# Recurrent branch: the order of TensorE's work in the state stage, around the norms and at the group starts

## The chip, the cores and the metric

The kernel runs on one core of a Trainium2 chip. The metric is the device time of one launch in microseconds (us); lower is better. The core's engines run separate instruction streams and meet at semaphores: PE is TensorE (matmuls), DVE is VectorE, ACT is ScalarE, POOL is GpSimd, SP issues most DMAs.

## The reference

Two layers of a hybrid trunk over 640 tokens (512 of a sample, 128 of a prompt), width 1024. Each layer projects its input, runs three branches (a recurrent one, gated linear attention, latent attention), merges them and projects back. The change lies in the recurrent branch, whose core is

```python
def step(s, inp):
    r_t, w_t, k_t, v_t, kk_t, a_t = inp
    sa = jnp.einsum('bhij,bhj->bhi', s, -kk_t)
    s = (s * w_t[:, :, None, :] + sa[..., None] * (kk_t * a_t)[:, :, None, :]
         + v_t[..., None] * k_t[:, :, None, :])
    return s, jnp.einsum('bhij,bhj->bhi', s, r_t)
...
o = outs[0] + outs[1]                      # two directions
mu = jnp.mean(o, -1, keepdims=True)
var = jnp.mean(jnp.square(o - mu), -1, keepdims=True)
o = (o - mu) * lax.rsqrt(var + RW_GN_EPS)
...
bonus = jnp.sum(r * k * r_k, -1, keepdims=True) * v
```

## The kernel before

The recurrence is computed in chunks of 128 tokens. A layer loops over 4 **pairs** of heads (p); each pair handles 5 **steps** (s = 0 to 3 of the sample, s = 4 the prompt), in both directions at once, in three **groups**: (0, 1), (2, 3) and (4,). Every engine's stream is written out by hand in one order; nothing is scheduled by a planner. Only PE's stream is touched by the change.

A pair goes like this on PE:

- **Opening.** `sums("kkss")` reduces the squared keys; it waits for `dve_kksq`, which DVE makes at the end of its work on the pair before. Projections of later inputs (`BESIDE[p]`, `project`, 8 weight tiles each) follow.
- **Group start.** `turns(s)` transposes B, K (result TB) and A, v (result TA) of a step; `scores(s, "Ab", B_)` and `scores(s, "Ak", K_)` make two score tiles of two PSUM banks each. DVE masks Ab twice: a small copy into XX (signal `dve_XT`, L1578) and two full copies (L1551), after which Ab's banks are free; it masks the XX parts of both steps first, then all of the first step's Ab, then the second step's Ab, then the first step's Ak. PE transposes XX back (result X, waits for `dve_XT`), and squares it (X2, X4, X8 ...), a chain that ACT and DVE empty from PSUM.
- **Solving.** V1, V2, V3, then Ya, Ye, Yb, each with an ACT or DVE copy between.
- **State stage.** For each step: TaT (a transpose), U (waits for `dve_state`, the running state), the state update S and the output O. S and O are sums over several matmuls; `open_outputs(s)` issues their first terms ahead, at a place where PE would wait. After the O of step 0 and of step 2, `turns` of the next group's first step is issued.
- **Closing.** `bonus`, `omean` and `ovar` are three norm sums, `ovar` waits for `dve_osq`, the squares that DVE makes from `omean`. Then comes the next pair's first projection, then the next `kkss`. After `ovar` ACT takes a logarithm and an exponential, and DVE five products and then the next pair's scaled keys and their square (`dve_kksq`).

`beat(r)` (r = 0 to 11) issues pieces of other projections in the prompt's group.

PSUM has 8 banks. `ticket` hands them out in a ring, in program order; banks of open sums are held and passed over. The matmul that takes a bank waits until the engine that reads the bank's last content is done with it. PE runs in order, so whatever is behind such a matmul waits as well. An order of matmuls is thus also an assignment of banks.

Of the kernel before, what the change touches and what calls it, by code (L numbers as in the profile page):

```python
# [30 lines left out]
P = 128  # L31
# [149 lines left out]
def build(nc, a, seen):  # L181
# [4 lines left out]
    with ctx:  # L186
# [311 lines left out]
        def _(pe):  # L498
# [103 lines left out]
            for l in range(DEPTH):  # L602
# [8 lines left out]
                pe.wait_ge(act_tanh.sem, act_tanh[l])  # L611
                for p in range(PAIRS):

                    project(l, BESIDE[p][0])
# [11 lines left out]
                    for steps in GROUPS:  # L626
# [78 lines left out]
                        def open_outputs(s):  # L705

                            TA, TB = B(s, "TA", 2), B(s, "TB")
                            got(s, ("TB", "act"))
                            opened["S", s] = ticket(pe, ("S", l, p, s), 1, "dve") if s != 3 else None
                            for d in range(2) if s != 3 else ():  # L710
                                mm(psum[:, opened["S", s] + P * d:opened["S", s] + P * d + P], TB[:, 2 * d + 1, :],
                                   TA[:, d, :], d == 0, False)
# [5 lines left out]
                            book["held"] |= {opened[k, s] // 512 for k in "SO" if opened[k, s] is not None}  # L718
# [23 lines left out]
                        for s in steps:  # L742
                            if s in (0, 1, 3):
                                turns(s)
                        for s in steps:
                            scores(s, "Ab", B_)
                        scores(steps[0], "Ak", K_)
                        beat(0)
                        for s in steps:
# [7 lines left out]
                            last.then_inc(filled.sem, filled.mark(("X", l, p, s)))  # L757
                        for s in steps:
# [55 lines left out]
                        open_outputs(steps[0])  # L814
# [5 lines left out]
                        for s in steps:  # L820
                            got(s, ("Ya", "act"), ("Ya", "dve"))
                            halves64(s, "Ye", "dve", 0, carried)
                        beat(10)
                        for s in steps:
                            got(s, ("Ye", "dve"))
                            halves64(s, "Yb", "act dve", 1, solved)
                        for s in steps:
# [8 lines left out]
                        for s in steps:  # L836
                            K, TA, TB = B(s, "K"), B(s, "TA", 2), B(s, "TB")
                            U = K[:, 2:4, :] if s != 4 else B(s, "J")[:, 2:4, :]
                            if s != 4:
# [9 lines left out]
                                if s + 1 in steps:  # L849
                                    open_outputs(s + 1)  # L850
                                got(s, ("U", "dve"))
                            at, s_at = opened["O", s], opened["S", s]
# [1185 lines left out]
```

## Time and profile before

| | us |
|---|---|
| median of 3 runs | 2876.14 (2874.84 to 2878.2) |
| the profiled execution: its time | 2874.18 |
| its span | 2872.4 |
| PE busy in the span | 2693.6 (94%) |
| DVE busy, ACT busy | 1180.9 (41%), 854.2 (30%) |
| recurrent branch, layer 0 | about 142 to 775 of the span |
| recurrent branch, layer 1 | about 1573 to 2138 of the span |

Where PE is idle inside its span, the profile names the engine whose signal ended the idle time. "Granted clock" is the share of 2.4 GHz that TensorE got; 0.50 is its lower level, 1.2 GHz.

### The profile page before, as it was taken

Reading aid. Unit: us, or ns where it says so; the run is one execution under the profiler, and the core shown is the slowest. Engines: PE = TensorE matmul, PEld = TensorE weight load, DVE = VectorE, ACT = ScalarE, POOL = GpSimd, SP = SyncE. Lnnn points to the kernel's source line nnn. Section 1 sums busy time; section 2 is a strip of 40 time slices with the busy share of each in tenths; the row PEclk is TensorE's granted clock in tenths of the full one; section 3 lists DMA queues with packets and bytes.
Section 4 is the critical chain, followed back from the end, with each engine's and each line's share of the span. In section 5 each row is a group of like instructions: output and inputs, shape, how many; then the busy total and the mean of one; then the engine's idle time right before and its main releaser. Section 6 shows DMA issues by size and latency. Waiting matters only on the chain.

```text
span 2872.4 us, 49516 instructions
## 1 busy us (share of the span) xinstructions
PE 2693.6 (94%) x21716; PEld 1726.2 (60%) x21716; DVE 1180.9 (41%) x2329; ACT 854.2 (30%) x1366; POOL 33.8 (1%) x62
## 2 busy tenths in 40 slices
PE   8999999999988999999999999999998899999997
PEld 2585756657555665555555858585755556555554
DVE  1452626454275454211134545454547644421112
ACT  1332314242244444200013232323324444420000
POOL 0000000000000000000000000000000000000000
PEclk9999999999999999999999999999999999999998
DMA  8101011020200100222231010101010010012221
GB/s 324 52 10 68 24 40 52 15 77 2 76 23 23 35 16 23 89 72 67 84 99 59 2 40 9 39 10 32 17 32 23 23 35 15 23 54 67 73 76 62
DMA packets 35844, 140.79 MB, mean 49 GB/s; under 512 B 4592, under 2 KB 4624, under 8 KB 35120
## 3 DMA queue, kind: packets, MB, share of 16 engines
q1 hardware_dynamic: 31968, 116.74, 12.6%
q0 software_dynamic: 3664, 20.88, 2.1%
q8 instruction: 175, 2.87, 0.4%
q14 instruction: 37, 0.30, 0.0%
HBM read 130.62 MB, written 6.98 MB: 48 GB/s over the span
## 4 chain that ended last, share of the span: by engine, by line
PE 82%; DVE 9%; ACT 6%; issue 2%; DMA 1%; POOL 0%; ACTq 0%; DVEq 0%; SPq 0%; POOLq 0%
PE psum L500 79%; PE psum L503 2%; DVE tmp L1401 1%; DVE tmp L1404 1%; DVE m_nm L1876 1%; DVE tmp L1412 1%; ACT tmp L1373 1%; DVE tmp L1578 1%; DVE acts L1401 1%; DVE tmp L1551 1%; ACT tmp L1126 1%; DVE acts L1404 1%; DMA ring<-units 1%; ACT acts L1126 1%; ACT L1121 0%
## 5 line engine op out<-in xcount | busy, mean ns | idle before, releaser
L500 PE MATMUL psum<-hT,ring 128*128 128x128 f32 (+1 forms) x3904 | 1127.2, 443 | 32.4 <-DVE acts L1404 22.6
L500 PEld LDWEIGHTS psum<-hT,ring 128*128 128x128 f32 x3904 | 613.6, 193 | 557.9 <-issue 521.7
L500 PE MATMUL psum<-tmp 64*64 64x64 f32 (+9 forms) x10624 | 706.9, 259 | 56.7 <-DVE tmp L1404 13.9
L500 PEld LDWEIGHTS psum<-tmp 64*64 64x64 f32 (+3 forms) x10624 | 555.6, 149 | 173.0 <-issue 60.5
L1126 ACT ACTIVATE tmp<-psum 128x512 f32<-128x512 f32 (+6 forms) x406 | 214.0, 530 | 570.2 <-PE psum L500 490.5
L500 PE MATMUL psum<-acts,ring 128*128 128x512 f32 (+1 forms) x768 | 210.8, 434 | 0.0
L1126 ACT ACTIVATE acts<-psum 128x640 f32<-128x640 f32 (+4 forms) x206 | 109.4, 531 | 336.5 <-PE psum L500 310.2
L1401 DVE TENSOR_TENSOR tmp<-psum,tmp 128x256 f32<-128x256 f32 (+2 forms) x184 | 75.7, 411 | 263.0 <-PE psum L500 224.7
L1404 DVE TENSOR_TENSOR tmp<-tmp,psum 128x640 f32<-128x640 f32 x32 | 26.3, 821 | 375.4 <-ACT tmp L1391 205.6
L500 PEld LDWEIGHTS psum<-acts,ring 128*128 128x128 f32 x768 | 117.3, 191 | 92.1 <-issue 92.1
L1391 ACT ACTIVATE tmp<-psum 128x640 f32<-128x640 f32 x32 | 22.5, 703 | 443.6 <-PE psum L500 443.6
L500 PE MATMUL psum<-tmp,ring 128*128 128x512 f32 (+1 forms) x512 | 138.8, 434 | 0.0
L503 PE MATMUL psum<-con_sb,tmp 128*128 128x128 f32 x696 | 107.3, 280 | 25.6 <-ACT tmp L1373 13.4
L500 PE MATMUL psum<-acts 64*64 64x64 f32 (+3 forms) x2448 | 111.9, 230 | 13.4 <-DVE acts L1404 7.5
L1401 DVE TENSOR_TENSOR tmp<-tmp 128x320 f32<-128x320 f32 (+2 forms) x198 | 117.7, 621 | 4.6
L500 PEld LDWEIGHTS psum<-tmp,ring 128*128 128x128 f32 x512 | 77.4, 191 | 61.2 <-issue 61.2
L1876 DVE TENSOR_REDUCE m_nm<-psum 128x1 f32<-128x768 f32 (+1 forms) x80 | 65.8, 823 | 104.2 <-PE psum L500 103.2
L500 PEld LDWEIGHTS psum<-acts 64*64 64x64 f32 (+2 forms) x2448 | 95.9, 140 | 19.7 <-DVE acts L1401 9.7
L503 PEld LDWEIGHTS psum<-con_sb,tmp 128*128 128x128 f32 x696 | 79.1, 141 | 47.0 <-DVE tmp L1408 27.8
L1404 DVE TENSOR_TENSOR tmp<-tmp,acts 128x320 f32<-128x320 f32 (+1 forms) x160 | 88.6, 586 | 42.8 <-ACT tmp L1313 37.0
L1551 DVE COPY_PREDICATED tmp<-masks_sb,psum 128x512 f32<-128x512 uint8 x160 | 105.2, 721 | 1.0 <-PE psum L500 0.2
L500 PE MATMUL psum<-ring,sc 128*2 128x512 f32 x192 | 95.1, 614 | 9.1 <-DMA ring<-units 9.1
(152 smaller groups left out, 1854.4 us busy)
## 6 DMA issues: line engine op xcount, KB each, us to landing
ring<-units SPq DMA_DIRECT2D x218, 512.0 KB, 3.5
small_sb<-small POOLq DMA_DIRECT2D x2, 2944.0 KB, 11.5
hT<-xT POOLq DMA_DIRECT2D x1, 2560.0 KB, 12.6
tmp<-xT POOLq DMA_DIRECT2D x8, 320.0 KB, 4.5
x_keep<-hT POOLq DMA_DIRECT2D x8, 320.0 KB, 4.7
tmp<-x_keep POOLq DMA_DIRECT2D x8, 320.0 KB, 3.5
yT<-acts POOLq DMA_DIRECT2D x8, 320.0 KB, 3.5
tmp<-masks SPq DMA_DIRECT2D x1, 1536.0 KB, 8.8
```

Source lines behind the costliest of these rows:

```text
L500: return nc.tensor.matmul(out, lhsT, rhs, start=start, stop=stop, skip_group_check=True)
L503: return nc.tensor.transpose(out, in_, ident[p, p])
L1126: nc.scalar.activation(out, src, ACT.Copy).then_inc(act_e.sem, act_e.mark(key))
L1373: nc.scalar.activation(m_p[n % 3][:, 0:w], psum[:, at:at + w], ACT.Exp, bias=m_nm[:, n:n + 1], accum_out=m_sum[:, n:n + 1]).then_inc(act_e ...
L1391: nc.scalar.activation(f_s[j], psum[:, at:at + T], ACT.Sigmoid).then_inc(act_e.sem, act_e.mark((key, l, n)))
L1401: return V.tensor_tensor(out, a, b, op)
L1404: return V.tensor_tensor(out, a, b, ALU.mult)
L1412: return V.scalar_tensor_tensor(out=out, in0=a, scalar=s, in1=b, op0=op0, op1=op1)
L1551: return V.copy_predicated(gbuf(s % 2, name, 4).rearrange("p (d h) x -> p d h x", d=2), masks[:, m, :, :].unsqueeze(2).broadcast_to([P, 2, ...
L1578: ins = V.copy_predicated(XX[cs, 0:4, :].rearrange("p (d h) x -> p d h x", d=2), masks[cs, M_XT, :, cs].unsqueeze(2).broadcast_to([64, 2, ...
L1876: V.reduce_max(m_nm[:, n:n + 1], psum[:, at:at + w], AX.X, negate=True).then_inc(dve_nm.sem, dve_nm.mark(l, h, i))
```

## The change

It moves PE instructions and removes none. (1) At a group start, the scores of the first step come before the second step's transposes, and X of the first step before Ak. (2) The next group's Ab scores follow its `turns` in the state stage. (3) `open_outputs` is split: the state's opening stays at its place for the first step and moves to behind Yb for the second; the output's opening moves to behind Ye for the first step. (4) In the closing, `beat(11)` moves ahead of `omean`, and the next pair's first projection is halved: 4 tiles between `omean` and `ovar`, 4 behind `ovar` (after the last pair it is the kvd projection).

```diff
+                project(l, BESIDE[0][0])
                 for p in range(PAIRS):
-                    project(l, BESIDE[p][0])
                     pe.wait_ge(dve_kksq.sem, dve_kksq[l, p])
...
-                        for s in steps:
-                            if s in (0, 1, 3):
-                                turns(s)
-                        for s in steps:
-                            scores(s, "Ab", B_)
-                        scores(steps[0], "Ak", K_)
-                        beat(0)
-                        for s in steps:
+                        def untransposed(s):
...
+                        if steps[0] == 0:
+                            turns(0)
+                            scores(0, "Ab", B_)
+                        for s in steps[1:]:
+                            scores(s, "Ab", B_)
+                            turns(s)
+                        beat(0)
+                        untransposed(steps[0])
+                        scores(steps[0], "Ak", K_)
+                        for s in steps[1:]:
+                            untransposed(s)
...
-                        open_outputs(steps[0])
+                        open_state(steps[0])
                         beat(8)
...
+                        open_output(steps[0])
                         beat(10)
...
+                        for s in steps[1:]:
+                            open_state(s)
...
                                 if s + 1 in steps:
-                                    open_outputs(s + 1)
+                                    open_output(s + 1)
...
                             if s in (0, 2):
                                 turns(s + 2)
+                                scores(s + 2, "Ab", B_)
...
+                    beat(11)
                     pe.wait_ge(dve_e.sem, dve_e[("O", l, p, 4)])
                     sums(("omean", l, p), bd, [item("k", p)], by="dve")
-                    beat(11)
+                    following = BESIDE[p + 1][0] if p + 1 < PAIRS else END_ITEMS[0]
+                    project_some(l, following, range(4))
                     pe.wait_ge(dve_osq.sem, dve_osq[l, p])
                     sums(("ovar", l, p), bd, [w_ys], by="act")
+                    project_some(l, following, range(4, KT))
...
-                for it in END_ITEMS:
-                    project(l, it)
```

**The group start.** This is PE's stream at the first group of layer 0's first pair before the change. The 128x256 matmuls are scores (Ab of step 0, Ab of step 1, Ak of step 0); the 64x64 ones from con_sb are X of step 0 and 1, the others X2 of step 0. `act_emptied` and `dve_emptied` are the signals for a free bank.

```order
L500 MATMUL psum<-tmp 128x256 [waits act_emptied]
L500 MATMUL psum<-tmp 128x256 x3
L500 MATMUL psum<-tmp 128x256 [waits dve_emptied]
L500 MATMUL psum<-tmp 128x256 x3
L500 MATMUL psum<-tmp 128x256 [waits act_emptied]
L500 MATMUL psum<-tmp 128x256 x3
L500 MATMUL psum<-con_sb,tmp 64x64 [waits act_emptied,dve_XT]
L500 MATMUL psum<-con_sb,tmp 64x64 x7
L500 MATMUL psum<-con_sb,tmp 64x64 [waits act_emptied,dve_XT]
L500 MATMUL psum<-con_sb,tmp 64x64 x7
L500 MATMUL psum<-tmp 64x64 [waits dve_emptied,act_emptied]
L500 MATMUL psum<-tmp 64x64 x15
```

And this is the same place now, from the second step's last transposes on.

```order
L503 MATMUL psum<-con_sb,tmp 128x128
L503 MATMUL psum<-con_sb,acts 128x128
L500 MATMUL psum<-con_sb,tmp 64x64 [waits act_emptied,dve_XT]
L500 MATMUL psum<-con_sb,tmp 64x64 x7
L500 MATMUL psum<-tmp 128x256 [waits dve_emptied,act_emptied]
L500 MATMUL psum<-tmp 128x256 x3
L500 MATMUL psum<-con_sb,tmp 64x64 [waits dve_emptied,dve_XT]
L500 MATMUL psum<-con_sb,tmp 64x64 x7
L500 MATMUL psum<-tmp 64x64 [waits dve_emptied,act_emptied]
L500 MATMUL psum<-tmp 64x64 x15
```

Ak now stands between the two X and waits for DVE as well, and so does the second X. Which content each bank held follows from replaying `ticket`: before, X2 of the first step took a bank of the first step's Ab (in the first and third pair of layer 0 and in all of layer 1); now Ak takes one of the first step's Ab, and X of the second step or X2 of the first takes one of the second step's Ab, in every pair.

**The closing.** PE's stream at the end of layer 0's first pair before (bonus and omean read acts and con_sb, the row of ring and sc and the hT rows behind it are `beat(11)`, then ovar, the projection, and kkss of the next pair):

```order
L500 MATMUL psum<-acts,con_sb 128x512 [waits dve_emptied]
L500 MATMUL psum<-acts,con_sb 128x128
L500 MATMUL psum<-ring,sc 2x512
L500 MATMUL psum<-hT,ring 128x512
L500 MATMUL psum<-hT,ring 128x128
L500 MATMUL psum<-hT,ring 128x512
L500 MATMUL psum<-hT,ring 128x128
L500 MATMUL psum<-tmp,con_sb 128x512 [waits dve_emptied,act_emptied,dve_osq]
L500 MATMUL psum<-tmp,con_sb 128x128
L500 MATMUL psum<-hT,ring 128x512 [waits dve_emptied,act_emptied,unit0_loaded]
L500 MATMUL psum<-hT,ring 128x512 x7
L500 MATMUL psum<-hT,ring 128x128 x8
```

And now, from ovar on (four tiles of the projection already stand ahead of it):

```order
L500 MATMUL psum<-tmp,con_sb 128x512 [waits dve_emptied,dve_osq]
L500 MATMUL psum<-tmp,con_sb 128x128
L500 MATMUL psum<-hT,ring 128x512
L500 MATMUL psum<-hT,ring 128x128
L500 MATMUL psum<-hT,ring 128x512
L500 MATMUL psum<-hT,ring 128x128
L500 MATMUL psum<-hT,ring 128x512
L500 MATMUL psum<-hT,ring 128x128
L500 MATMUL psum<-hT,ring 128x512
L500 MATMUL psum<-hT,ring 128x128
L500 MATMUL psum<-tmp,con_sb 128x512 [waits dve_emptied,dve_kksq]
L500 MATMUL psum<-tmp,con_sb 128x128
```

Between ovar and kkss there were 8 tiles of a projection; now there are 4.

## Rows read from the trace of the kernel before

**Rows 1.** The page, part 1: busy time, share, instructions.
```profile
PE 2693.6 (94%) x21716; PEld 1726.2 (60%) x21716; DVE 1180.9 (41%) x2329; ACT 854.2 (30%) x1366; POOL 33.8 (1%) x62
```

**Rows 2.** Windows, PE: stretch, length, busy, granted clock; layer 1's recurrent branch.
```profile
1573.00:2138.00 565.00, 540.64 (x6978) 1.00 0.07 22
```

**Rows 3.** Timeline, PE, group start, layer 1: start, length; idle time ahead.
```profile
1573.22 0.71 PE L503 MATMUL psum<-con_sb,tmp 128*128 128x128 f32 x5
...
1575.06 2.86 PE L500 MATMUL psum<-tmp 64*128 64x256 f32 x24
...
1579.59 3.51 PE L500 MATMUL psum<-tmp 64*64 64x64 f32 x112 [0.60 <-DVE tmp L1551]
```

**Rows 4.** Timeline, DVE, the same group start.
```profile
1576.24 1.84 DVE L1578 COPY_PREDICATED tmp<-masks_sb,psum 64x256 f32<-64x256 uint8 x4 [1.16 <-PE psum L500]
1578.11 1.34 DVE L1551 COPY_PREDICATED tmp<-masks_sb,psum 128x512 f32<-128x512 uint8 x2
...
1580.01 2.57 DVE L1551 COPY_PREDICATED tmp<-masks_sb,psum 128x512 f32<-128x512 uint8 x4
```

**Rows 5.** Timeline, PE, from Yb to the second group's X2.
```profile
1600.19 0.65 PE L500 MATMUL psum<-tmp 64*64 64x128 f32 x8 [0.52 <-DVE tmp L1401]
...
1604.74 1.30 PE L500 MATMUL psum<-tmp 128*128 128x128 f32 x12
...
1607.42 0.68 PE L500 MATMUL psum<-tmp,acts 128*128 128x128 f32 x4 [0.35 <-DVE acts L1401]
...
1608.62 0.71 PE L500 MATMUL psum<-acts 128*128 128x128 f32 x4
...
1615.41 3.50 PE L500 MATMUL psum<-tmp 64*64 64x64 f32 x112 [0.60 <-DVE tmp L1551]
```

**Rows 6.** Timeline, DVE: the O of step 1 is added.
```profile
1610.66 0.48 DVE L1401 TENSOR_TENSOR acts<-acts,psum 128x128 f32<-128x128 f32 x2
```

**Rows 7.** Timeline, then windows of PE, second group, layer 0, second pair.
```profile
344.00 0.71 PE L500 MATMUL psum<-acts 128*128 128x128 f32 x4
...
351.18 1.91 PE L500 MATMUL psum<-tmp 64*128 64x256 f32 x8 [2.50 <-DVE tmp L1551]
...
354.78 3.45 PE L500 MATMUL psum<-tmp 64*64 64x64 f32 x112
...
352.00:353.00 1.00, 1.00 (x6) 0.50 0.00 0
```

**Rows 8.** Timeline, PE: step 2's S and the prompt's X2, layers 0 and 1.
```profile
379.41 1.30 PE L500 MATMUL psum<-tmp 128*128 128x128 f32 x12
...
390.07 1.15 PE L500 MATMUL psum<-tmp 64*64 64x64 f32 x32 [0.48 <-ACT tmp L1126]
...
1640.11 1.30 PE L500 MATMUL psum<-tmp 128*128 128x128 f32 x12
...
1648.37 1.15 PE L500 MATMUL psum<-tmp 64*64 64x64 f32 x32 [0.48 <-ACT tmp L1126]
```

**Rows 9.** Timeline, the closing: layer 1 on PE and DVE, then one row of layer 0.
```profile
1676.84 2.40 PE L500 MATMUL psum<-acts,con_sb 128*128 128x512 f32 x8 [0.21 <-DVE tmp L1412]
...
1682.29 1.32 PE L500 MATMUL psum<-tmp,con_sb 128*128 128x512 f32 x4 [0.89 <-ACT acts L1126]
1683.44 8.82 PE L500 MATMUL psum<-hT,ring 128*128 128x512 f32 x32
1692.10 1.25 PE L500 MATMUL psum<-tmp,con_sb 128*128 128x512 f32 x4
...
1690.33 0.83 DVE L1404 TENSOR_TENSOR tmp<-tmp 128x640 f32<-128x640 f32 x1
...
261.71 1.32 PE L500 MATMUL psum<-acts,con_sb 128*128 128x512 f32 x4 [1.01 <-DVE tmp L1404]
```

**Rows 10.** Timeline and windows, PE: an idle time elsewhere and the clock.
```profile
2153.88 2.50 PE L500 MATMUL psum<-acts 64*128 64x128 f32 x20 [3.76 <-DVE acts L1404]
...
2154.00:2156.00 2.00, 2.00 (x20) 0.50 0.00 0
```

More of the change, by code:

```diff
@@ L703, in _, with open_state, open_output @@
                         opened = {}
-                        def open_outputs(s):
+                        def open_state(s):
+                            if s == 3:
+                                return
                             TA, TB = B(s, "TA", 2), B(s, "TB")
                             got(s, ("TB", "act"))
[L709 to L712, printed above, removed]
+                            opened["S", s] = at = ticket(pe, ("S", l, p, s), 1, "dve")
+                            for d in range(2):
+                                mm(psum[:, at + P * d:at + P * d + P], TB[:, 2 * d + 1, :], TA[:, d, :], d == 0, False)
+                            book["held"].add(at // 512)
+                        def open_output(s):
+                            TA = B(s, "TA", 2)
                             opened["O", s] = at = ticket(pe, ("O", l, p, s), 1, "dve")
@@ L717, in open_outputs @@
                                    d == 0, False)
-                            book["held"] |= {opened[k, s] // 512 for k in "SO" if opened[k, s] is not None}
+                            book["held"].add(at // 512)
                         def halves64(s, key, by, second, lhsT_at):
@@ L849, in _ @@
                                 if s + 1 in steps:
-                                    open_outputs(s + 1)
+                                    open_output(s + 1)
                                 got(s, ("U", "dve"))
-                            at, s_at = opened["O", s], opened["S", s]
+                            at, s_at = opened["O", s], opened.get(("S", s))
                             for d in range(2) if s != 3 else ():
@@ L863, in _ @@
                             last.then_inc(filled.sem, filled.mark(("O", l, p, s)))
-                            book["held"] -= {opened[k, s] // 512 for k in "SO" if opened[k, s] is not None}
+                            book["held"].discard(at // 512)
+                            if s != 3:
+                                book["held"].discard(s_at // 512)
                             if s in (0, 2):
                                 turns(s + 2)
+                                scores(s + 2, "Ab", B_)
                     pe.wait_ge(dve_rkr.sem, dve_rkr[l, p])
                     sums(("bonus", l, p), bd, [item("r", p)], by="dve")
+                    beat(11)
                     pe.wait_ge(dve_e.sem, dve_e[("O", l, p, 4)])
                     sums(("omean", l, p), bd, [item("k", p)], by="dve")
-                    beat(11)
+                    following = BESIDE[p + 1][0] if p + 1 < PAIRS else END_ITEMS[0]
+                    project_some(l, following, range(4))
                     pe.wait_ge(dve_osq.sem, dve_osq[l, p])
                     sums(("ovar", l, p), bd, [w_ys], by="act")
+                    project_some(l, following, range(4, KT))
                 if l + 1 < DEPTH:
                     mod_turn(l + 1, MOD_GROUPS - 1)
-                for it in END_ITEMS:
-                    project(l, it)
                 filling = [0]
```

## The prediction

> **What bounds the kernel now.** I read the page's busy times first: PE is busy 94% of the span, DVE 41% [rows 1]. So the kernel is a PE program with gaps, and a reordering that adds no matmul can only win or lose gaps. The windows put 24.4 us of gaps in layer 1's recurrent branch (565.00 less 540.64) at full clock [rows 2]: some 6 us in each pair. Then I read the timeline of one pair and asked of each gap which engine ended it. In a pair of layer 1 they are: before X2 in both full groups (0.60 each, DVE masking) [rows 3, 5]; behind Ye (0.52, DVE) and before U of step 1 (0.35, DVE) [rows 5]; before the prompt's X2 (0.48) [rows 8]; and 0.21 and 0.89 in the closing [rows 9]. All are shorter than 1 us. The reader is to see that there is little to win per gap, and that wherever a matmul is moved, the waits of its PSUM bank move too. I price each pair as the shift of a landmark, since PE is nearly gapless between landmarks.
>
> **(1) Group start.** In layer 1 the transposes start at 1573.22 and the scores at 1575.06, so one step's transposes take 0.92 [rows 3]. DVE begins to mask 1.18 after the scores start, needs 1.84 for both XX parts, then 1.34 for the first Ab, and after two short adds it starts the second Ab at 1580.01; of that row's four copies the first two, half of 2.57, are that Ab: done at 1581.30, 6.24 after the scores [rows 3, 4]. X2 started 4.53 after the scores, as soon as the first Ab's bank was free, 6.37 after the first transpose [rows 3]. Now the scores start 0.92 earlier, but X2 (or the X ahead of it) takes a bank of the second Ab: 0.92 + 6.24 + about 0.15 of signalling = 7.3 after the first transpose, so 0.95 later. What lies ahead (2.0 us of Ab scores, 0.92 of transposes, 1.5 of Ak and X) fits in between. Where it is X of step 1 that waits (second pair of layer 1), its own 0.55 comes behind the wait: 1.5. In layer 0's second and fourth pairs one bank is held and before already had longer waits; I take 0.55. Queued behind the wait is all of PE. Sum: 5 x 0.95 + 1.5 + 2 x 0.55 = 7.4 us slower.
>
> **(2, 3) State stage and second group.** The output's opening takes 0.58 (8 short matmul records) and now fills the 0.52 behind Ye, and the state's opening (0.45) mostly a wait for ACT before the second TaT: S of step 0 starts 0.75 earlier. U of step 1 then waits for PE itself: about 1.2 of S and O, 0.92 of turns and 0.97 of Ab scores are 3.1 after S, against 2.68 before (1604.74 to 1607.42) [rows 5]. Step 1's S thus starts 0.3 earlier, with Ab of step 2 behind it. But Ab of step 3 takes a bank of the O of step 1, free only when DVE has added it (1611.14, 2.52 after step 1's S started; PE sees it at 2.66) [rows 5, 6], while PE is through at 1.25: a new gap of 1.4. DVE starts XX of step 3 at 3.85, and the second Ab is masked 0.91 + 1.34 + 0.65 + 1.29 later, at 8.05 [rows 4]. X2 follows at 8.2 to 8.3; before it came 6.79 after step 1's S (1608.62 to 1615.41) [rows 5]. Net, with the 0.3: 1.1 slower in six pairs. In layer 0's second and fourth pairs before had the 2.50 wait and X2 came 10.8 after that S (344.0 to 354.78), part of it at the lower clock [rows 7]; by the same count it comes at 8.7, and step 1's S 0.65 later: 1.45 faster each. Sum: 6.6 - 2.9 = 3.7 slower.
>
> **Third group.** The second group's opening gains 0.58 [rows 5]. In six pairs TB of the prompt now takes the bank of step 2's O: by 2.66 after S instead of 1.2 [rows 5, 6], then turns, Ab and U. Counted through (U at 4.3, O done at 6.1, one tile 1.28, X at 7.8, Ak, X2) X2 comes 9.35 after step 2's S against 8.26 before [rows 8]: +1.1 - 0.58 = 0.5 slower. In the two pairs with a held bank it comes at 9.0 against 10.66 [rows 8]: 2.2 faster. Sum: 3.0 - 4.4 = 1.4 faster. The parts so far: 7.4 + 3.7 - 1.4 = 9.7 slower.
>
> **(4) Closing.** This is the firmest term. From the start of ovar at 1682.29 ACT and DVE need until 1691.16 for the squared keys of the next pair (1690.33 + 0.83), 8.9 us [rows 9]. kkss waits for them and all of PE stands behind kkss. Before, ovar (1.15) and eight tiles (8.66) covered this: kkss started at 1692.10, 9.81 after ovar, without a wait [rows 9]. Now ovar and four tiles cover 1.15 + 4.33 = 5.5. A wait of 3.4 appears at six boundaries. In exchange the 0.89 before ovar goes (four tiles stand there) [rows 9]; in layer 0 also the 1.01 before omean [rows 9], less a wait for O at the bonus in one pair. Net 2.5 in layer 1, about 2 in layer 0: 3 x 2.5 + 3 x 2 = 13.5. After the last pair of a layer no kkss comes, but the DVE chain behind ovar continues into the gated branch; bounds 0 and 3.4 each, I take 0.5, since the kkss part of the chain is missing: 1 us.
>
> **The clock.** An idle time of 3.76 was followed by 0.50 of the clock, that is 1.2 GHz, in the next stretch; so was one of 2.50 [rows 7, 10]. A wait of 3.4 after a fully busy PE lies nearer to the first two. The scores of the 2.50 case took 1.91 for 8 records where 24 took 2.86 [rows 3, 7]: 0.9 lost on them alone, and another 0.8 on what follows until X2. I take 1.7 per boundary, six boundaries: 10 us. Bounds 0 and 10.
>
> The Trainium skill, "TensorE: Matmul & The Clock Gate", section "HAM oscillation — how this bites in real kernels", says that idle times repeated in every turn of a loop make the clock fall again in each turn; the trace agrees with the 3.76 row and its 0.50, and by that rule all six boundaries pay.
>
> **Sum.** 9.7 + 14.5 + 10 = 34 slower. The profiled execution took 2874.18, its span 2872.4; it lies within the runs (2874.84 to 2878.2 around 2876.14) but for 0.7. 2874.18 + 34 = 2908; the median stands 2 above it: 2909.
>
> **The rivals.**
> *The clock holds at the boundaries* (0.15). For it: 3.4 is shorter than 3.76. Against it: 2.50 was enough [rows 7]. 9.7 + 14.5: 2899.
> *The clock falls at group starts too* (0.10). There are 16 starts with two or three gaps of 0.6 to 1.5 close together. Against it: layer 1's recurrent branch, with gaps of 0.6 at its starts, ran at 1.00 throughout [rows 2, 3]. Eight of them at 1.7 add 13: 2922. The same page, section "A second HAM failure mode: psum-queue depth-cycling", has the clock fall where PE idles briefly but often for PSUM banks; the trace of before does not show it at gaps of 0.6 [rows 2].
> *The inner order wins* (0.10), the case on the other side. Its mechanism: DVE gets Ab up to 0.9 earlier at each start. If bank waits didn't bind behind it, all inner gaps would go: 0.60 x 2 + 0.52 x 2 + 0.35 + 0.48 = 3.1 a pair, 25 over 8 pairs, and 3.6 twice for the 2.50 wait and its clock, together 32 against a closing of 24.5: 2869. It decides once the inner gain is over 24.5 (14.5 if the clock holds). Against it: in the new stream of the group start Ak and the second X wait for DVE's emptying, which they did not before.
> *No effect* (0.08): the closing's wait is as computed but the inner gaps pay for it, as between the last two: 2876.
> Forecast, 0.57: 2909.
>
> **Chances and range.** A measurement here tells a change from none above about 0.2%, 5.8 us. The inner case gives 0.08 faster and 0.02 same; no effect gives 0.05 same and 0.03 slower; the rest is slower. Faster 0.08, same 0.07, slower 0.85. The range reaches down below 2899 for inner terms sized wrong by up to 10 (each start by 0.6), and up to 2922: 2886 to 2922. The forecast's own range is 2900 to 2918.
>
> **What would show it.** Right: six PE waits of 3.1 to 3.7 for DVE before kkss, with 0.50 of the clock behind; DVE waits (L1551) of 0.6 to 1.2 at 16 group starts, now before Ak and before the second X or X2; none before ovar and 0.5 less behind Ye. Wrong: kkss waits under 2 us, which would mean that ovar starts earlier than four tiles allow; or X2 at the old distance from the first transpose, which would mean that the second Ab's bank is not what ends the wait.

## The result, and the profile after

The changed kernel takes 2909.24 us (median of 4 runs, 2905.12 to 2914.79); before takes 2875.49 beside it (4 runs, 2872.16 to 2878.2). The ratio is 1.0119, with a 95% interval from 1.0096 to 1.0142. The profiled execution took 2906.18, its span is 2904.4, 32.0 more than before's. Forecast was 2909, slower. One execution of before, beside experiments 5 to 8, ran in a slower state of the chip (3492.01) and isn't counted in any ratio.

The page's busy line answers to [rows 1]. PE's busy time grew by 12 without one matmul more, and its idle time by 20:

```profile
PE 2705.6 (93%) x21716; PEld 1724.7 (59%) x21716; DVE 1181.3 (41%) x2329; ACT 853.5 (29%) x1366; POOL 33.8 (1%) x62
```

The closing of layer 1's first pair, timeline of PE, which answers to [rows 9]: the prompt's last products, bonus, beat(11), omean, four tiles, ovar, four tiles, kkss. Lines of `kernel.py` have moved by 18. A row of a timeline is one group of matmuls; the last row of a view is cut off where the view ends, so its length and count can be short.

```profile
1689.28 1.27 PE L500 MATMUL psum<-tmp 128*128 128x128 f32 x12 [0.48 <-DVE tmp L1589]
1690.76 1.32 PE L500 MATMUL psum<-acts,con_sb 128*128 128x512 f32 x4 [0.21 <-DVE tmp L1430]
1691.91 2.33 PE L500 MATMUL psum<-hT,ring 128*128 128x512 f32 x8
1694.08 1.25 PE L500 MATMUL psum<-acts,con_sb 128*128 128x512 f32 x4
1695.16 4.49 PE L500 MATMUL psum<-hT,ring 128*128 128x512 f32 x16
1699.49 1.25 PE L500 MATMUL psum<-tmp,con_sb 128*128 128x512 f32 x4
1700.57 4.49 PE L500 MATMUL psum<-hT,ring 128*128 128x512 f32 x16
1708.34 1.35 PE L500 MATMUL psum<-tmp,con_sb 128*128 128x512 f32 x4 [3.29 <-DVE tmp L1422]
```

The 0.89 before ovar is gone, and kkss waits 3.29 for DVE: it starts 8.85 after ovar. A boundary is this place between two pairs of one layer; there are six. The same timeline at four more of them:

```profile
283.77 2.50 PE L500 MATMUL psum<-tmp,con_sb 128*128 128x512 f32 x4 [3.28 <-DVE tmp L1422]
...
452.06 2.50 PE L500 MATMUL psum<-tmp,con_sb 128*128 128x512 f32 x4 [3.28 <-DVE tmp L1422]
...
621.41 2.34 PE L500 MATMUL psum<-tmp,con_sb 128*128 128x512 f32 x4 [3.29 <-DVE tmp L1422]
...
1863.18 1.66 PE L500 MATMUL psum<-tmp,con_sb 128*128 128x512 f32 x4 [3.28 <-DVE tmp L1422]
```

(The sixth, at 2019.27, waits 3.28 too.) The waits are alike, what follows is not: the same four matmuls take 1.35 here and 2.50 there. The windows around the six (columns: length; busy time of PE, PEld, DVE, ACT and POOL; granted clock; DMA share and GB/s) say why:

```profile
283.00:289.00 6.00, 5.23 (x15) 2.69 (x16) 1.53 (x2) 1.82 (x2) 0.00 (x0) 0.72 0.07 28
449.00:458.00 9.00, 5.94 (x14) 3.00 (x15) 3.73 (x5) 4.32 (x5) 0.00 (x0) 0.62 0.18 60
620.00:626.00 6.00, 4.59 (x13) 2.36 (x14) 2.15 (x3) 1.50 (x3) 0.00 (x0) 0.72 0.16 63
1708.00:1714.00 6.00, 5.66 (x19) 2.82 (x20) 1.62 (x3) 3.37 (x4) 0.00 (x0) 1.00 0.00 0
1862.00:1868.00 6.00, 4.82 (x14) 2.58 (x15) 1.91 (x3) 2.24 (x3) 0.00 (x0) 0.72 0.14 55
2019.00:2025.00 6.00, 5.73 (x20) 2.88 (x21) 1.62 (x3) 3.44 (x4) 0.00 (x0) 1.00 0.00 1
```

The clock fell to 1.2 GHz at four boundaries and stayed at 2.4 at two. A drop takes at most the length times what is missing to 1.00: 6 x 0.28 = 1.7 at three of them, 9 x 0.38 = 3.4 at the second, where the drop came double. That is the most it can cost, since what falls into the wait itself costs nothing.

The start of group (0, 1) in layer 1, PE and then DVE, answers to [rows 3, 4]: transposes 0, Ab 0 and 1, transposes 1, X 0, Ak 0, X 1, X2.

```profile
1584.07 0.71 PE L503 MATMUL psum<-con_sb,tmp 128*128 128x128 f32 x5
...
1585.04 2.00 PE L500 MATMUL psum<-tmp 64*128 64x256 f32 x16
1586.96 0.77 PE L503 MATMUL psum<-con_sb,tmp 128*128 128x128 f32 x5
...
1587.99 0.68 PE L500 MATMUL psum<-con_sb,tmp 64*64 64x64 f32 x16
1589.58 1.13 PE L500 MATMUL psum<-tmp 64*128 64x256 f32 x8 [0.91 <-DVE tmp L1569]
1590.64 0.68 PE L500 MATMUL psum<-con_sb,tmp 64*64 64x64 f32 x16
1591.48 0.74 PE L500 MATMUL psum<-tmp 64*64 64x64 f32 x18
...
1588.09 1.34 DVE L1569 COPY_PREDICATED tmp<-masks_sb,psum 128x512 f32<-128x512 uint8 x2
...
1589.99 2.56 DVE L1569 COPY_PREDICATED tmp<-masks_sb,psum 128x512 f32<-128x512 uint8 x4
```

X2 starts 7.41 after the first transpose; before it was 6.37. Ak waits 0.91 for the bank of the first Ab, which is masked at 1588.09 + 1.34 = 1589.43.

The state stage and the third group, PE, answer to [rows 5, 8]: step 1's S, Ab of step 3, its transposes, Ak of step 2, X of step 3, X2; then the prompt's transposes.

```profile
1620.55 0.71 PE L500 MATMUL psum<-acts 128*128 128x128 f32 x4
...
1623.23 1.13 PE L500 MATMUL psum<-tmp 64*128 64x256 f32 x8 [1.38 <-DVE acts L1419]
...
1626.74 1.13 PE L500 MATMUL psum<-tmp 64*128 64x256 f32 x8 [0.74 <-DVE tmp L1569]
1627.80 0.68 PE L500 MATMUL psum<-con_sb,tmp 64*64 64x64 f32 x16
1628.72 1.46 PE L500 MATMUL psum<-tmp 64*64 64x64 f32 x43 [0.23 <-DVE tmp L1569]
...
1655.39 0.66 PE L503 MATMUL psum<-con_sb,tmp 128*128 128x128 f32 x4 [1.29 <-DVE acts L1419]
```

Ab of step 3 stands 1.38 behind the bank of step 1's output, X2 comes 8.17 after step 1's S, and the prompt's transposes stand 1.29 behind the bank of step 2's output.

**Where the 32.0 are.** Time from one kkss to the next (start to start, from the two timelines), with the prediction's terms for the same stretch summed. A drop of the clock behind a kkss lengthens the stretch that begins there, so its 1.7 stands with the pair behind the boundary:

| stretch | before | after | more | predicted |
|---|---|---|---|---|
| layer 0, pair 1 | 161.80 | 167.71 | 5.9 | 4.55 |
| layer 0, pair 2 | 168.52 | 168.29 | -0.2 | 0.6 |
| layer 0, pair 3 | 162.24 | 169.35 | 7.1 | 6.25 |
| layer 0, pair 4, to the end of the gated branch's wait | 184.10 | 181.82 | -2.3 | -0.9 |
| layer 1, pair 1 | 148.89 | 154.27 | 5.4 | 5.05 |
| layer 1, pair 2 | 148.87 | 154.84 | 6.0 | 7.3 |
| layer 1, pair 3 | 148.89 | 156.09 | 7.2 | 6.75 |
| layer 1, pair 4, to the same wait's end | 164.02 | 167.94 | 3.9 | 4.75 |
| all the rest | | | -1.0 | 0 |

The same 33.0 by part of a pair, summed over the eight pairs, from landmark to landmark in the two timelines:

| part of a pair | predicted | measured |
|---|---|---|
| kkss to the first transpose (the clock) | 10 | 6.8 |
| first transpose to the first X2 (group start) | 7.4 | 8.6 |
| to X2 of the second group | 3.7 | 6.0 |
| to the prompt's X2 | -1.4 | -1.7 |
| to the prompt's last products | 0 | 1.3 |
| to kkss, or to the end of the gated branch's wait (closing) | 14.5 | 12.0 |

### The profile page after: what moved, and what is told of

It reads as the page before. It is cut to its first block, busy times and chain, and to the rows that moved or that the text cites. A ratio compares the mean times of both kernels' runs of the same rounds, so it can differ in the third digit from the quotient of the medians.

```text
span 2904.4 us, 49482 instructions
## 1 busy us (share of the span) xinstructions
PE 2705.6 (93%) x21716; PEld 1724.7 (59%) x21716; DVE 1181.3 (41%) x2329; ACT 853.5 (29%) x1366; POOL 33.8 (1%) x62
## 4 chain that ended last, share of the span: by engine, by line
PE 80%; DVE 11%; ACT 6%; issue 2%; DMA 1%; POOL 0%; ACTq 0%; DVEq 0%; SPq 0%; POOLq 0%
PE psum L500 78%; PE psum L503 2%; DVE tmp L1419 2%; DVE tmp L1569 1%; DVE tmp L1422 1%; DVE tmp L1430 1%; DVE acts L1419 1%; DVE m_nm L1894 1%; ACT tmp L1391 1%; ACT L1139 1%; DVE acts L1422 1%; ACT tmp L1144 1%; DMA ring<-units 1%; DVE tmp L1426 0%; DVE tmp L1596 0%
```

## The experiments

Each was timed 4 to 11 times, and the kernel before beside it on the same chip; the ratio is to before, with its 95% interval. A kernel with one part "alone" is the kernel before with that one part. Waits, windows and drops of the clock are those of one profiled execution of each kernel.

**1. The closing alone.** Beside the new place of `project(l, BESIDE[0][0])` ahead of the loop:

```diff
+                    beat(11)
                     pe.wait_ge(dve_e.sem, dve_e[("O", l, p, 4)])
                     sums(("omean", l, p), bd, [item("k", p)], by="dve")
-                    beat(11)
+                    project_some(l, following, range(4))
                     pe.wait_ge(dve_osq.sem, dve_osq[l, p])
                     sums(("ovar", l, p), bd, [w_ys], by="act")
+                    project_some(l, following, range(4, KT))
```

> The kernel before with only the new closing: the last beat ahead of omean, four tiles of the next item ahead of ovar and four behind. Main theory (the closing carries about two thirds of the loss): kkss waits 3.3 for DVE at six boundaries, no wait before ovar; by the landmarks of the changed kernel's trace (behind the prompt's U to kkss) 2.3 slower at three boundaries of layer 1 and 1.9 at three of layer 0, 12.7, about 1 each for the last pairs, and 1.5 to 2 at each boundary at which the clock falls (4 to 6 of them), 6 to 12: 2875.5 + 22 = 2897, between 2894 and 2902. Rival A (the boundary is cheap, the inner order carries the 33): under 2885. Rival B (closing and inner order only hurt together, since waits of the one reach into the other): under 2885 here and no loss in the kernel with the inner order alone.

Measured: 2894.36, ratio 1.0077 [1.0065, 1.009], 21 more. The timeline of PE at two boundaries:

```profile
278.58 2.01 PE L500 MATMUL psum<-tmp,con_sb 128*128 128x512 f32 x4 [3.28 <-DVE tmp L1405]
...
451.10 1.35 PE L500 MATMUL psum<-tmp,con_sb 128*128 128x512 f32 x4 [3.28 <-DVE tmp L1405]
```

The wait is there at all six, and the clock fell behind four of them again, but not the same four: here the one at 451 kept it and the one at 2008 lost it, and the double drop came at the third (615). The closing carries two thirds of the loss; rivals A and B fall.

**2. The inner order alone.** The changed kernel with the old closing (the diff of 1 taken back).

> The changed kernel with the old closing: group starts, openings and early scores as changed. Main theory: the rest of the 33, about 10 slower than before: 2885, between 2880 and 2891; no drop of the clock at the boundaries, waits of 0.7 to 1.4 behind the group starts and before Ab of step 3. If the parts are independent, its loss and that of the closing alone add up to 33 within 4. Rival (the inner order wins by itself and the closing hides it): 2869 or less.

Measured: 2882.14, ratio 1.0037 [1.0023, 1.0051]: 9 to 11 more. No boundary drops the clock. 0.77% and 0.37% add up to 1.14% for the 1.19% of the whole change: within the intervals the two parts simply add. By kkss and ovar times, layer 0's first and third pairs are 3.6 and 2.4 slower and its second and fourth, where before had the waits of 2.50, 4.8 and 5.0 faster; layer 1's are 3.1 to 3.5 slower.

**3. The openings alone.**

```diff
-                        open_outputs(steps[0])
+                        open_state(steps[0])
                         beat(8)
...
                             halves64(s, "Ye", "dve", 0, carried)
+                        open_output(steps[0])
...
                             halves64(s, "Yb", "act dve", 1, solved)
+                        for s in steps[1:]:
+                            open_state(s)
...
-                                    open_outputs(s + 1)
+                                    open_output(s + 1)
```

> The kernel before with only the openings parted: the state's before Yb's end and the output's behind Ye, nothing else moved. Main theory: the output's opening (0.58) fills the 0.52 behind Ye and the state's opening part of a wait before TaT, so that S of the first step starts 0.75 earlier in each first group and 0.58 in each second one: 8 x 1.3 = 10.6 faster, 2865, between 2860 and 2870. The inner loss of the change is then what is left over a gain of 10: about 20 for the moved scores and group starts. Rival (U and S wait for DVE whatever PE does ahead of them): same as before, 2872 to 2878, with the waits before U or S longer by as much.

Measured: 2859.72, ratio 0.9955 [0.9942, 0.9967]: 13 faster. The number fits, the reason doesn't. A pair of layer 1 (ovar at 1669.47 to ovar at 1818.38) takes 148.91, before 148.87: nothing gained. The timeline of PE in layer 1 shows what ate the 1.3:

```profile
1601.32 0.68 PE L500 MATMUL psum<-con_sb,tmp 64*64 64x64 f32 x16 [1.04 <-DVE tmp L1562]
...
1603.21 1.00 PE L500 MATMUL psum<-tmp 64*64 64x64 f32 x27 [0.28 <-DVE tmp L1562]
...
1628.95 0.66 PE L503 MATMUL psum<-con_sb,tmp 128*128 128x128 f32 x4 [1.28 <-DVE acts L1412]
```

X and X2 of step 3 now get banks of Ab, and the prompt's transposes the bank of the output of step 2. The gain is in layer 0's second and fourth pairs (5.1 and 7.0 by the ovar times; the third has 1.2), whose waits of 2.50 [rows 7] are 1.66 and 1.05 here, without the two drops of the clock. The likely reason is another place in the ring of banks and not a filled gap; this run alone doesn't show it, experiment 5 shows that banks alone can do as much.

**4. The start of group (0, 1) alone.** The kernel before; only its first group goes transposes 0, Ab 0 and 1, transposes 1, X 0, Ak 0, X 1.

> The kernel before with only the start of group (0, 1) in the changed order: transposes 0, Ab 0, Ab 1, transposes 1, X 0, Ak 0, X 1; the other groups as before. Main theory (X2 can't start until DVE has emptied the second Ab, whose scores start no earlier relative to DVE's work): X2 0.95 later after the first transpose in five pairs, 1.5 in one, 0.55 in two, 7.4 slower: 2883, between 2879 and 2887. Rival (DVE starts its masking 0.9 earlier and X2 follows it): 5 to 8 faster, 2868 to 2871.

Measured: 2879.03, ratio 1.0023 [1.0014, 1.0032]: 6 slower, 7.4 predicted. The profiled execution is the slowest of the eleven (2883.55). In it layer 1's first two pairs are 1.0 longer each. The third is 3.4 longer: right behind its start, with waits of 0.82 before Ak and 0.84 before the second X (1882.67), PE had this window at half speed:

```profile
1883.00:1886.00 3.00, 3.00 (x62) 3.00 (x60) 0.74 (x2) 0.86 (x2) 0.00 (x0) 0.50 0.00 0
```

So the rival "the clock falls at group starts too" can happen; in the profiled execution of the changed kernel it did at none of them.

**5. The openings, with the bank of the output kept back.** Experiment 3, and one line moved:

```diff
-                            book["held"].discard(at // 512)
                             if s != 3:
                                 book["held"].discard(s_at // 512)
                             if s in (0, 2):
                                 turns(s + 2)
+                            book["held"].discard(at // 512)
```

> The parted openings alone, and the bank of each output kept out of the ring until the next unit's transposes are issued, so that these take another bank. It is for the kernel with the openings alone, whose trace shows layer 1 no faster than before (its pairs are 148.9 long in both) and a new wait of 1.28 for DVE before the prompt's transposes and one of 1.04 plus 0.28 before the second X and X2 of group (2, 3). Theory (the openings' 1.3 a pair is real, and the bank that comes free last eats it): the 1.28 goes, the waits at the start of group (2, 3) fall back to the 0.60 of before, each pair of layer 1 is 1 to 1.5 shorter: 2860 less 6 to 10, 2852. Rival (PE waits there for what DVE computes, and the bank is only where it shows): 2857 to 2862, the same idle time at another place.

Measured: 2850.11, ratio 0.9917 [0.9904, 0.993]: 10 to 11 faster than experiment 3, 24 faster than before. The 1.28 is gone, both X run without a wait, and beside 0.35 before the first Ab (1590.77) this is the only wait left at the start of group (2, 3):

```profile
1595.29 2.90 PE L500 MATMUL psum<-tmp 64*64 64x64 f32 x91 [0.58 <-DVE tmp L1562]
```

Layer 1's pairs are 147.4 to 148.3 long for 148.9. The order of PE's instructions is that of experiment 3; only the banks differ. The rival (PE waits there for what DVE computes, 2857 to 2862) falls.

**6. Three tiles ahead of ovar, five behind** (the changed kernel, `range(3)` and `range(3, KT)`).

> The changed kernel with three tiles of the next item ahead of ovar and five behind (it has four and four). DVE's squares take 3.04 after omean's start, omean and three tiles 4.42, so ovar waits for nothing; kkss is ready 8.85 after ovar, of which PE covers 1.15 and 5 x 1.08: the wait before kkss is 2.2 for 3.28, and each of six boundaries is 1.08 shorter: 2909 less 6.5, 2902, if the clock does as before. Theory (a wait of 2.2 no longer drops the clock): another 5 to 7 off, 2896. Rival (2.2 drops it in as many boundaries as 3.28 did, 4 of 6): 2902. Rival B (the price is not the wait but that ovar comes late): no change to 2909.

Measured: 2893.33, ratio 1.0067 [1.0054, 1.008]: 16 faster than the changed kernel with 1.08 less wait at each boundary. The wait before kkss is 2.20 at all six. The clock fell at the three of layer 0 and at none of layer 1; two windows, one of each:

```profile
449.00:455.00 6.00, 5.52 (x15) 2.74 (x16) 1.62 (x3) 3.55 (x5) 0.00 (x0) 0.72 0.20 78
...
1700.00:1706.00 6.00, 5.49 (x19) 2.82 (x20) 1.62 (x3) 3.55 (x5) 0.00 (x0) 1.00 0.19 75
```

Neither theory holds whole. Between the two profiled executions 10.5 is gone, and can be followed: 6 x 1.08 of wait, 1.7 at the second boundary, whose drop is single here, and 1.7 in layer 1, which has none. The medians say 15 to 16. The rest is which executions were profiled: the changed kernel's is 3.1 below its median, this one's 2.4 above, and within each kernel the slower executions have the lower mean clock (0.984 to 0.980 there, 0.986 to 0.984 here).

**7. Openings, and three choices of banks.** Experiment 5, X2 in the bank of its own X, and ovar kept off the bank of the item just projected:

```diff
-                            at = ticket(pe, ("X2", l, p, s), 1, "act")
+                            at = same(pe, ("X", l, p, s), ("X2", l, p, s), "act")
...
+                    kept = {grown["item_at"] // 512, grown["item_at"] // 512 + 1} - book["held"]
+                    book["held"] |= kept
                     sums(("ovar", l, p), bd, [w_ys], by="act")
+                    book["held"] -= kept
```

`same` sets the ring to the old key's bank, takes the ticket and sets the ring back.

> The openings with the late bank, and two more changes of banks alone: X2 takes the bank of its own X (PE waits for ACT to have emptied that anyway), and ovar may not take the bank of the item just projected (before, it waits 0.89 for ACT to empty it at six or more boundaries). No instruction of PE stands elsewhere than with the openings alone. Theory (many of PE's short waits are for a bank, not for data): 0.60 twice a pair and 0.89 at six boundaries go: 9.6 and 5.3 less than with the late bank alone, about 2838, and 2835 to 2846 if part of it comes back before X4 and GT. Rival (DVE's chain of masks is the bound and the wait moves to X4, GT or X8): 2850 or more.

Measured: 2843.66, ratio 0.9894 [0.9878, 0.9909]: the fastest, 30 under before and some 65 under the changed kernel. Layer 1's pairs are 145.4 to 146.3 long. The closing of its first pair: ovar, eight tiles, kkss, no wait at all.

```profile
1664.11 1.25 PE L508 MATMUL psum<-tmp,con_sb 128*128 128x512 f32 x4
1665.19 8.82 PE L508 MATMUL psum<-hT,ring 128*128 128x512 f32 x32
1673.89 1.35 PE L508 MATMUL psum<-tmp,con_sb 128*128 128x512 f32 x4
```

It is some 6 short of what the expectation counted. Layer 0's second pair became 163.1 for 161.4; and from the last ovar through the gated branch, where no line was changed, it took 5.4 more in layer 0 and 1.1 in layer 1. The 5.4 go with the clock, not with waits: PE's waits there are those of experiment 5 to 1.2 in sum (29.0 for 27.8), but of the 200 us from the branch's first wait on the granted clock is 0.92 here and 0.95 in experiment 5, which is 6. The two windows, first here, then in experiment 5:

```profile
773.00:973.00 200.00, 173.85 (x1212) 117.77 (x1213) 120.74 (x237) 88.42 (x103) 2.88 (x5) 0.92 0.08 26
...
775.00:975.00 200.00, 175.14 (x1237) 118.17 (x1238) 124.52 (x243) 90.63 (x106) 3.45 (x6) 0.95 0.09 28
```

**8. The start alone, X2 in the bank of its X** (experiment 4 with `same` for steps 0 and 1).

> The kernel with the new start of group (0, 1) alone (2879), and X2 of that group in the bank of its own X. Theory of the prediction (what ends the wait before X2 is the bank of the second Ab): X2 follows X at once, 0.3 to 0.9 earlier per pair and 3 to 7 off in eight pairs: 2873 to 2876, back at the kernel before. Rival (the 0.91 before Ak, which waits for the bank of the first Ab, is the whole loss, and X2 gains nothing from another bank): 2877 to 2880.

Measured: 2873.66, ratio 0.9996 [0.9987, 1.0005]: no loss left that can be told. But the trace splits it (PE, layer 1, first transpose at 1572.04; Ak, X 1, X2):

```profile
1577.56 1.13 PE L508 MATMUL psum<-tmp 64*128 64x256 f32 x8 [0.91 <-DVE tmp L1573]
1578.62 0.68 PE L508 MATMUL psum<-con_sb,tmp 64*64 64x64 f32 x16
1579.13 1.04 PE L508 MATMUL psum<-tmp 64*64 64x64 f32 x30
```

X2 comes 7.09 after the first transpose for 7.41: the bank of the second Ab is worth 0.3, and layer 1's pairs are 149.5 long, 0.4 under experiment 4 and 0.65 over before. What is left is the first Ab's bank. Before, X2 itself took it, at 6.37. Now Ak takes it and starts 5.52 after the first transpose, when it comes free, and Ak and the second X, 1.57, stand between it and X2: 7.09. (No run gave Ak another bank, so this half is read from the trace and not tested.) In the two profiled executions the rest of the difference goes with the clock: experiment 4's had four drops in its recurrent branches, this one none. Both theories hold in part.

This trace also has the wait of 2.50 of [rows 7], before the same matmuls. Here the clock didn't fall behind it, nor behind its like at 682:

```profile
351.48 0.88 PE L508 MATMUL psum<-tmp 64*128 64x256 f32 x5 [2.50 <-DVE tmp L1573]
...
351.00:357.00 6.00, 5.50 (x152) 5.06 (x154) 3.45 (x7) 2.13 (x5) 0.00 (x0) 1.00 0.01 3
```

**9. The early scores.** The changed kernel with the old closing and the old start of group (0, 1):

```diff
                         if steps[0] == 0:
-                            turns(0)
-                            scores(0, "Ab", B_)
-                        for s in steps[1:]:
-                            scores(s, "Ab", B_)
-                            turns(s)
+                            for s in steps:
+                                turns(s)
+                            for s in steps:
+                                scores(s, "Ab", B_)
...
```

> The changed kernel with the old closing and the old start of group (0, 1): what stays are the parted openings, the scores Ab of steps 2 and 4 issued in the state stage, and the new start of groups (2, 3) and the prompt. Theory (the early scores take the loss: Ab of step 3 stands behind the bank of step 1's output, 1.4, and X2 comes no earlier for it): the inner kernel's 2882 less the 6.6 of the start alone, 2875.5, between 2872 and 2879, that is 15 above the openings alone (2860). Rival (the start of group (0, 1) makes the inner loss and the early scores cost nothing): 2865 or less.

Measured: 2873.28, ratio 1.0002 [0.9993, 1.001]: 13 to 14 above the openings alone. The wait before Ab of step 3 is 1.38 here as well (1604.52), and X2 comes 8.16 after step 1's S. The early scores, with the start of the later groups that goes with them, cost what the openings gain.

**10. Six tiles ahead, two behind** (`range(6)`, `range(6, KT)`).

> The changed kernel with six tiles ahead of ovar and two behind. Each of six boundaries is 2 x 1.08 longer and the wait before kkss is 8.85 less 1.15 and 2.17, 5.5 for 3.28: 2909 + 13, and the last pairs' ovar 2.2 later each, up to 4 more: 2922 to 2926 if the clock does as before. Theory (a longer wait drops the clock at every boundary; 2.20 did at 3, 3.28 at 4 of 6): 2 drops of 1.7 more, 2925 to 2930. Rival (what decides the clock is not the length of the wait): 4 of 6 again. Rival B (the two tiles ahead of ovar hide something, the loss is less than 2.17 a boundary): under 2918.

Measured: 2929.23, ratio 1.0194 [1.018, 1.0208], 20 more than the changed kernel, as the theory had it. The wait is 5.44 at all six, and the clock fell at all six, at half speed through the whole of kkss (2.50 where it took 1.35 at full speed); five of the six drops came double. Three of the windows:

```profile
284.00:290.00 6.00, 4.46 (x10) 2.19 (x12) 2.24 (x4) 1.05 (x2) 0.00 (x0) 0.50 0.00 0
...
1715.00:1721.00 6.00, 3.80 (x8) 1.88 (x10) 2.90 (x4) 0.40 (x1) 0.00 (x0) 0.72 0.00 0
...
2033.00:2042.00 9.00, 6.75 (x15) 3.40 (x16) 3.40 (x5) 3.31 (x4) 0.00 (x0) 0.62 0.00 0
```

**11. Experiment 5 and ovar's bank** (experiment 7 without `same`).

> The parted openings with the late bank of the output, and ovar kept off the bank of the item just projected. Theory (the 0.89 before ovar is for a bank that ACT empties, and DVE's squares are ready 3.04 after omean, before PE is there at 3.34): 0.89 less at six or seven pairs, 2850 less 5 to 6, 2845, the fastest with the order of PE's groups as before. Rival (the banks of later groups shift by one and bring waits back elsewhere, as in the kernel with the own bank for X2, where layer 0's pairs were 160.2 and 163.1 long instead of 159.4 and 161.4): 2848 to 2853.

Measured: 2849.06, ratio 0.9915 [0.9901, 0.9928]: no different from experiment 5. Layer 1's pairs did become shorter (146.2 to 146.3 for 147.4 to 148.3), but layer 0's second pair went from 161.4 to 163.3, its fourth lost 2.2 (a wait of 2.52 at 670.8 where experiment 5 has 1.05, and a drop of the clock behind it), and layer 0's gated branch took 2.1 more, at a granted clock of 0.93 (778 to 978) for 0.95. The rival held in the two pairs; in the gated branch it is the clock.

**12. All eight tiles behind ovar**, the beat still ahead of omean.

> The changed kernel with all eight tiles of the next item behind ovar, the beat still ahead of omean. From omean's start: squares ready at 3.04, so ovar waits 2.0 behind omean's 1.17; kkss could start 8.85 after ovar and PE is there at 9.81: no wait there. From omean to kkss 13.0 for 14.26: six boundaries 1.2 shorter, 2909 less 7.5, and ovar of the last pairs 2.2 earlier, up to 4 off: 2898 to 2902 with the clock as before. Theory (a gap of 2.0 drops the clock as often as the 2.20 before kkss did, 3 of 6): 2893 to 2897, as with three tiles ahead. Rival (eight tiles behind keep PE busy so that the clock never falls): under 2891.

Measured: 2895.86, ratio 1.0079 [1.0066, 1.0093], 2.5 above three and five, which the intervals don't tell apart. The wait stands before ovar now, 1.85 at every pair, none before kkss, and the clock fell at the three boundaries of layer 0, at none of layer 1. A wait of 1.85 ahead of ovar and one of 2.20 behind it are worth nearly the same, in time and in what they do to the clock.

## Why the prediction was right, point by point

**What bounds the kernel.** Right in the main: PE's count of matmuls is the same, and 20 of the 32 are idle time. Of the 12 that PE is longer busy, about 5 are half-speed stretches in the two recurrent branches (17.1 us of them after, 6.8 before). Blocks cut into shorter ones add some: in layer 1 PE's own pieces up to X2 fill 6.2 in the new order (experiment 8, 7.09 less its one wait) and filled 5.8 (6.37 less 0.60).

**(1) Group start.** The new distance was predicted as 7.3 and is 7.41; alone it costs 6 for 7.4 (experiment 4), in the changed kernel's trace 8.6: layer 0's second and fourth pairs came to 0.95 and 0.97 for the 0.55 that was taken without a count. The mechanism was named too narrowly. The prediction had the bank of the second Ab end the wait; experiment 8 gives it 0.3 of 1.0, and the other 0.65 are the first Ab's bank, which now holds up Ak with the second X behind it.

**(2, 3) State stage and second group.** This term is undersized, 6.0 for 3.7. The distance from step 1's S to X2 is right (8.2 to 8.3 predicted, 8.17 measured; 1.4 before Ab of step 3, 1.38 measured), but where that S starts is not. In layer 1's first pair, counted from the work ahead of the openings, S of step 0 came 0.58 earlier for 0.75, and U of step 1 3.32 after it for 3.1: step 1's S starts 0.1 later and not 0.3 earlier. In five second groups (all of layer 0, the third pair of layer 1) it was the first X that waited, 1.44 for DVE, where 0.6 to 1.2 before Ak had been named. What the parts would be worth alone I had not asked, and my expectation of experiment 3 got the openings from the wrong place. Measured alone, the openings are worth 13 and the early scores 13 the other way.

**Third group.** The 1.29 before the prompt's transposes is the predicted wait for the bank of step 2's output, in the six pairs named. 1.7 faster for 1.4.

**The inner sum** was 9.7; experiment 2 shows 9 to 11. In the changed kernel's trace its three parts make 12.9, of which about 3.5 come back in the closing: the waits of 0.8 and 1.0 there that layer 0's second and fourth pairs had before are gone by the inner order alone (experiment 2 has them no more). "The inner order wins" (0.10) is refuted by it.

**(4) Closing.** The wait is 3.28 for 3.4. From the prompt's last products to kkss it is 2.3 longer at the three boundaries of layer 1 (16.74 to 19.06 at the first), for 2.5, and 1.9, 1.5 and 1.3 at those of layer 0 (18.88 to 20.76 at the first), for 2 each. For the last pairs I took 0.5 each. The DVE chain behind ovar goes on into the gated branch, and the wait there is 5.73 in layer 0 and 5.65 in layer 1 for 3.76, 1.9 more:

```profile
803.23 2.50 PE L500 MATMUL psum<-acts 64*128 64x128 f32 x20 [5.73 <-DVE acts L1422]
```

But other waits ahead of it went, as the 0.89 before ovar in layer 1 and 0.8 and 1.0 in layer 0. Net, to the end of that wait, it is 0.8 longer in layer 1 and 0.45 shorter in layer 0. The whole closing is 12.0 for 14.5.

**The clock.** 1.7 for a single drop was right: layer 1's third pair, with a drop behind its kkss, is 1.8 longer than the first, which has none. "All six boundaries" was the step that failed. Four paid, one of them double: by the windows 1.7 + 3.4 + 1.7 + 1.7 = 8.5 at most, for 10. By the stretches behind kkss it is 6.8: a sixth of the double drop lies in the wait, and in layer 0's second and fourth pairs PE had a wait of 1.09 for ACT right behind (290.79 and 621.54 before), which is 0.59 and 0.38 now. One leg of the argument doesn't stand either: 2.50 "was enough" in before [rows 7], and in experiment 8 it wasn't, twice. The rule of the Trainium skill, "TensorE: Matmul & The Clock Gate", section "HAM oscillation — how this bites in real kernels", by which the clock falls again in each turn of a loop, agrees only with the longer wait: at 5.44 all six fell, at 3.28 four of six in either kernel that had it, at 2.20 and at 1.85 three.

**The signs.** Of those named for right, six waits of 3.1 to 3.7 before kkss, none before ovar and 0.5 less behind Ye are there; the clock behind them fell at four of the six; the waits at the starts of the first groups lie in 0.6 to 1.2, those of five second groups don't (1.44). None of the signs for wrong showed.

**The sum.** 34 predicted, 32.0 between the two spans and 33.8 between the medians. The mechanisms are the predicted ones and each row of the first table is within 1.4 of its own, but that the whole is within 2 is luck in part. The terms miss both ways and cancel: 3.2 too little for the three inner parts and 1.3 for a stretch put at nothing, 2.5 too much for the closing and 3.2 for the clock, and 1.0 gained elsewhere.

## What to carry to other kernels

Price a reordering by two questions for every instruction moved: which wait's cover is taken away, and which PSUM bank does its ticket now get, from whom. A ring that hands out banks in order makes both change at once, and banks can be chosen by themselves: on top of the openings, which gave 13 and were the best order tried, other banks under the same order of PE gave 10 to 11 more (experiment 5) and 16 to 18 more (experiment 7). Where two chains must be bridged by the same filler, count the filler against the longer one: kkss can start 8.85 after ovar, and ovar's own 1.15 with seven tiles of 1.08 are just short of that. The wait of 0.89 before ovar that four of them removed was for a bank.

## What the runs showed of the hardware

The drop of TensorE's clock behind an idle time is no matter of the idle time's length alone. In the profiled executions, inside the recurrent branches:

| wait of PE | the clock fell behind it | where |
|---|---|---|
| 5.44 | 6 of 6 | experiment 10 |
| 3.28 | 4 of 6 and 4 of 6 | changed kernel, experiment 1 |
| 2.50 | 2 of 2, 2 of 2, 1 of 1, 0 of 2 | before, experiments 1, 11 and 8 |
| 2.20 | 3 of 6, all in layer 0 | experiment 6 |
| 1.85 | 3 of 8, all in layer 0 | experiment 12 |
| 1.66 | 0 of 5 | experiments 1, 3, 5, 7 and 11 |

The 3.28 stand before the same four matmuls, and in the two kernels different boundaries paid. The other drops came behind a single wait of 1.38 (experiment 9 twice, experiment 10 once) or behind two waits close together: 1.44 and 1.11, or 0.80 and 1.01 (experiment 4), 0.82 and 0.84 (experiments 4 and 12). All of these waits also stand in traces without a drop; experiments 2, 3, 5, 7 and 8 have none in a recurrent branch. A single drop took up to 1.7, a double one up to 3.4.

What selects them is open: no run here varied that by itself. Nor is it fixed by the kernel: the four executions of the changed kernel had mean granted clocks of 0.984, 0.983, 0.981 and 0.980 at 2905.12, 2906.18, 2912.30 and 2914.79 us. 0.004 of the span is 12 us, so most or all of the 9.7 between them can be the clock, and which boundaries paid is known of one execution only. "A second HAM failure mode: psum-queue depth-cycling" on the page "TensorE: Matmul & The Clock Gate" of the Trainium skill, which has the clock fall where PE idles briefly but often for PSUM banks, fits the drops behind 0.82 and 0.84; since the same pairs of waits dropped nothing in experiments 2 and 8, it was a rival at 0.10 that is rare rather than absent.
